# Gate and up projections of three four-tile blocks by seven block products instead of eight, on one core

## What is computed

```python
h = _rmsnorm(x, g_pre_mix) * (1 + sc1) + sh1
proj = h @ w_in                                  # 1024 -> 2176 columns, 17 units of 128
ya = pool_mixer(xa) ; yb = conformer_conv(xb) ; yc = short_conv(xc)
mix = jnp.concatenate([ya, yb, yc], axis=-1) @ w_out       # 1024 -> 1024
x = x + gt1 * _rmsnorm(mix, g_post_mix)
h = _rmsnorm(x, g_pre_ffn) * (1 + sc2) + sh2
f = (jax.nn.silu(h @ w_gate) * (h @ w_up)) @ w_down        # 1024 -> 2816 -> 1024
x = x + gt2 * _rmsnorm(f, g_post_ffn)
```

## Time and profile before

| | |
|---|---|
| median of 3 runs | 2252.78 us (2251.18 to 2254.14) |
| the profiled execution | 2248.84 us |
| its span, first to last instruction | 2247.1 us |
| mean granted TensorE clock | 0.999 |
| TensorE, VectorE, ScalarE busy | 99%, 61%, 45% of the span |
| DMA | 376.8 MB, mean 168 GB/s |

### The profile page before, as it was taken

One profiled execution on the slowest core, in us unless ns is written; L12 is line 12 of the kernel. 1 busy time (PEld: TensorE's weight loads), 2 busy tenths in 40 slices (PEclk: granted clock), 3 DMA queues, 4 the chain that ended last, 5 costly groups with the idle time before them and its releaser, 6 DMA issues.

```text
span 2247.1 us, 29845 instructions
## 1 busy us (share of the span) xinstructions
PE 2227.4 (99%) x12150; PEld 2057.5 (92%) x12150; DVE 1366.5 (61%) x1982; ACT 1004.6 (45%) x1419; POOL 37.0 (2%) x83
## 2 busy tenths in 40 slices
PE   9999999999999999999999999999999999999998
PEld 6779998979999988999898899989899998799987
DVE  3779966798444678644478854357884535443343
ACT  3455466454344544344444525354443424532332
POOL 0000000000000000000000000000000000000000
PEclk9999999999999999999999999999999999999999
DMA  9865654654543564544365363437435434744332
GB/s 376 311 218 169 237 205 142 187 180 168 169 157 125 175 162 131 182 151 155 126 196 147 124 214 122 152 130 205 133 131 178 124 130 154 183 152 158 124 129 94
DMA packets 165765, 376.83 MB, mean 168 GB/s; under 512 B 75351, under 2 KB 77527, under 8 KB 165116
## 3 DMA queue, kind: packets, MB, share of 16 engines
q1 hardware_dynamic: 165630, 374.93, 51.1%
HBM read 348.02 MB, written 19.00 MB: 163 GB/s over the span
## 4 chain that ended last, share of the span: by engine, by line
PE 89%; DVE 4%; DMA 1%; ACT 1%; issue 0%; SPq 0%; DVEq 0%; ACTq 0%
PE ps L711 88%; DVE wlo L1445 2%; DVE pr L1607 1%; DMA raw<-in_w_dn 1%; DMA raw<-in_w_mix 1%; DVE early L1607 1%; PE ps L741 0%; DVE g_lo L1508 0%; ACT whi L1038 0%; DMA raw<-in_w_gu 0%; DVE h_lo L1498 0%; SPq L528 0%; ACT h_f L1112 0%; DVE xt L1525 0%; ACT junk L1061 0%
## 5 line engine op out<-in xcount | busy, mean ns | idle before, releaser
L1445 DVE TENSOR_TENSOR wlo<-raw,whi 128x1024 fp32r<-128x1024 f32 x531 | 647.3, 1223 | 567.0 <-ACT whi L1038 565.3
L1038 ACT ACTIVATE whi<-raw 128x1024 fp32r<-128x1024 f32 x531 | 561.7, 1059 | 950.0 <-DMA raw<-in_w_gu 562.2
L711 PE MATMUL ps<-h_hi,whi 128*128 128x384 f32 (+1 forms) x2808 | 920.9, 328 | 1.8 <-DVE h_lo L1501 1.1
L711 PE MATMUL ps<-h_hi,wlo 128*128 128x384 f32 (+1 forms) x2808 | 919.3, 327 | 0.0
L711 PE MATMUL ps<-h_lo,whi 128*128 128x384 f32 (+1 forms) x2808 | 919.2, 327 | 0.0
L711 PEld LDWEIGHTS ps<-h_hi,whi 128*128 128x128 f32 x2808 | 528.6, 188 | 7.1 <-issue 4.7
L711 PEld LDWEIGHTS ps<-h_lo,whi 128*128 128x128 f32 x2808 | 528.6, 188 | 0.5
L711 PEld LDWEIGHTS ps<-h_hi,wlo 128*128 128x128 f32 x2808 | 528.6, 188 | 0.0
L711 PE MATMUL ps<-whi,g_hi 128*128 128x512 f32 x748 | 232.2, 392 | 5.9 <-DVE g_lo L1508 4.9
L711 PE MATMUL ps<-wlo,g_hi 128*128 128x512 f32 x748 | 230.5, 389 | 0.0
L711 PE MATMUL ps<-whi,g_lo 128*128 128x512 f32 x748 | 230.5, 389 | 0.0
(11 more groups left out here) (152 smaller groups left out, 1229.6 us busy)
## 6 DMA issues: line engine op xcount, KB each, us to landing
raw<-in_w_gu SPq DMA_DIRECT2D x264, 512.0 KB, 3.3
raw<-in_w_mix SPq DMA_DIRECT2D x150, 512.0 KB, 3.3
raw<-in_w_dn SPq DMA_DIRECT2D x132, 512.0 KB, 3.3
xr<-in_x_all SPq DMA_DIRECT2D x29, 512.0 KB, 6.0
xr<-x_all SPq DMA_DIRECT2D x17, 512.0 KB, 5.9
pre<-in_w_ada SPq DMA_DIRECT2D x16, 512.0 KB, 10.6
x_all<-xr SPq DMA_DIRECT2D x5, 1536.0 KB, 7.7
xt<-turn SPq DMA_DIRECT2D x80, 96.0 KB, 4.5
```

What stands on the lines that cost most here:

```text
L711: return nc.tensor.matmul(out, lhsT, rhs, start=start, stop=stop, skip_group_check=True)
L1038: nc.scalar.activation(whi[:, s, :], raw[:, s, :], ACT.Copy).then_inc(w_hi, 1)
L1445: tt(wlo[:, s, :], raw[:, s, :], whi[:, s, :].bitcast(F32), ALU.subtract).then_inc(w_lo, 1)
```

## The change

1. **Blocks.** `NT` = 2, 3, 4, 4, 4; five blocks. A block of four tiles has 512 columns. `RING` = 5, `LEAD` = 3. `IN_DOWN`, `IN_GATE_UP` and the places of the statistics change; a 512 column block of sums fills all eight banks.
2. **Gate and up of the four-tile blocks.** The 22 steps of two units become 11 pairs of seven products. A pair is two gate and two up column blocks; weights and activations are cut in two along the contraction (`KH` = 4 chunks) and the tokens in two (`HALF` = 256). Each of the seven products takes one unit of weights (a quarter of gate and of up, or one of four sums S1 to S4) and one of seven token combinations (`c_hi`, `c_lo`), 2 x 12 matmuls of 256 columns. Partial sums stay in three bank pairs (A, C, B) and go on accumulating; VectorE adds them (`r1`, `u2`, `u3`), ScalarE copies and does the silus.
3. **Weight sums.** While block 1 does gate and up, VectorE makes S1 to S4 from the raw units of two steps (`weight_sums`) and SP stores 2 MB for each pair (`store_sums`); the blocks 2 to 4 load them.
4. **Token combinations.** In the down projection before, ScalarE and VectorE make seven pairs `c_hi`, `c_lo` and four differences (`HIGH_AT`, `LOW_AT`), instead of eight `h_hi`, `h_lo`.
5. **FFN activations through memory.** The products go to `g_out`, SP stores them to `g_mem` and loads chunk by chunk into a ring of four (`load_g`), one 128x512 chunk beside each down unit.
6. **Pooling map folded.** s_pool, w_pool and the two units of w_out behind them are multiplied once (`fold_pool`), stored, and loaded as two units (`w_fold`); the two `w_pool` matmuls of each block and their copies go away. `norm_rows` moves from the output projection into the gate/up stage.

```diff
-TB = 3
-NT = [2, 3, 3, 3, 3, 3]
+TB = 4
+NT = [2, 3, 4, 4, 4]
+PRODUCTS = [("A11", "11", "A"), ("S2", "T2", "B"), ("S1", "T1", "C"), ("S3", "T3", "B"),
+            ("A12", "21", "A"), ("S4", "22", "C"), ("A22", "T4", "B")]
+CHAIN_BANK = {"A": 0, "C": 2, "B": 4}
-RING = 6
+RING = 5
-LEAD = 4
+LEAD = 3
-    STREAM += [("gu", c_, m_, i_) for m_ in range(NF) for i_ in range(2)]
+    if sliced(c_):
+        STREAM += [("sg", c_, p_, i_) for p_ in range(PAIRS) for i_ in range(NPROD)]
+    else:
+        STREAM += [("gu", c_, m_, i_) for m_ in range(NF) for i_ in range(2)]
-IN_DOWN = 3
-IN_GATE_UP = [6, 6, 6, 6, 6]
+IN_DOWN = [None, 1, 2, 3]
+IN_GATE_UP = [6, 3, 1, 1]
 def sum_bank(r, t):
-            return 0 if r == RES.index(("mix", NB - 1)) and t == 0 else 2 + 2 * t
+            return (0, 2, 6, 4)[t] if sliced(RES[r][1]) else 2 + 2 * t
+            def load_g(b, k):
...
+                if at >= G_LAND:
+                    sp.wait_ge(g_lo_ready, at - G_LAND + 1)
+                sp.dma_start(down_rings(b)[0][:, at % G_LAND, 0:w], g_mem[b % 2, k, :, 0:w]).then_inc(gf_landed[at % G_LAND], 16)
+            def fold_pool(p):
...
+                for h in range(2):
+                    last = mm(ps[:, 6 + h, :], w_pl[:, p, :], fold[:, p, 512 * h:512 * h + 512], True, True)
+            def product(b, p, i):
+                n, at = UNIT["sg", b, p, i], pair_at(b, p)
+                s, combo_at, f = n % RING, COMBOS.index(PRODUCTS[i][1]), norm("F", b)
+                for g in range(2):
...
+                    elif i == 0 and p:
+                        pe.wait_ge(g11_ready if g else s11_ready, at)
+                    elif i == 1 and p:
+                        pe.wait_ge(v21_ready, 2 * at - 1 + g)
+                    elif i == 2 and p:
+                        pe.wait_ge(v12_ready, 2 * at - 1 + g)
+                    elif i == 3:
+                        pe.wait_ge(u2_ready, 2 * at + 1 + g)
+                    elif i == 4:
+                        pe.wait_ge(r1_ready, 2 * at + 1 + g)
+                    elif i == 5:
+                        pe.wait_ge(v22_ready, 2 * at + 1 + g)
+                    elif i == 6:
+                        pe.wait_ge(u3_ready, 2 * at + 1 + g)
...
+                    for k in range(KH):
+                        w = slice((KH * g + k) * P, (KH * g + k + 1) * P)
+                        mm(out, whi[:, s, w], c_hi[:, combo_at, k, :], i < 3 and k == 0, False)
+                        mm(out, whi[:, s, w], c_lo[:, combo_at, k, :], False, False)
+                        last = mm(out, wlo[:, s, w], c_hi[:, combo_at, k, :], False, k == KH - 1)
+            def weight_sums(n):
+                _, _, m, e = STREAM[n]
+                n2 = UNIT["gu", SUMMED, m + 1, e]
...
+                elif e == 0:
+                    dve.wait_ge(sums_stored, 16 * p)
+                dve.wait_ge(w_landed[n % RING], landed(n))
+                dve.wait_ge(w_landed[n2 % RING], landed(n2))
...
+                at = own.step(tt(s1, a21, a22, ALU.add))
+                own.step(tt(s3, a11, a21, ALU.subtract))
+                after(at)
+                after(own.step(tt(s2, s1, a11, ALU.subtract)))
+                i = tt(s4, a12, s2, ALU.subtract)
             def low(n):
                 s = n % RING
+                if STREAM[n][0:2] == ("gu", SUMMED) and STREAM[n][2] % 2 == 0:
+                    weight_sums(n)
```

More of the change, by code:

```diff
@@ L57 @@
 NY1 = NPOOL + NSC
-RING = 6
+RING = 5
 G_RING = 3
-LEAD = 4
+G_LAND = 4
+LEAD = 3
 EARLY = 6
@@ L222, in tile_order @@
     kind, b = RES[r]
[L223 to L229, removed]
+    return {2: [0, 1], 3: [1, 0, 2] if kind == "ffn" else [0, 1, 2], 4: [0, 3, 1, 2] if kind == "ffn" else [0, 1, 2, 3]}[NT[b]]
+BY_TILE = [r for r in range(len(RES)) if sliced(RES[r][1])]
 def tile_ends(r, i):
-    return (NT[NB - 1] - 1) * BY_TILE.index(r) + i + 1
+    return (TB - 1) * BY_TILE.index(r) + i + 1
 def res_tile(r, t):
@@ L507, in source @@
                     return w_mix[key[2]]
+                if key[0] == "out" and Y[key[2]][0] == "g":
+                    return w_fold[Y[key[2]][1]]
                 if key[0] == "out":
@@ L576, in _ @@
                         sp.dma_start(w_pl[h:h + 64, g // 2, h:h + 64], w_pool[g]).then_inc(w_pool_landed, 16)
+                if j == 13:
+                    for p in range(NPOOL):
+                        sp.dma_start(fold[:, p, :], w_mix[NIN + Y.index(("g", p))]).then_inc(fold_landed, 16)
                 if j == 10:
@@ L627, in _ @@
                     load("out", c, k)
+                    if c and sliced(c - 1) and k == 6:
+                        store_pair(c - 1, PAIRS - 1)
+                    if c and not sliced(c - 1) and 2 <= k < 5:
+                        store_chunk(c - 1, NF - 5 + k)
+                    if c == SUMMED + 1 and k == 0:
+                        store_sums(PAIRS - 1)
                     if c == 0 and k == 1:
@@ new lines, in down @@
+                order = tile_order(r)
+                if ks[0] == 0 and sliced(b) and b < NB - 1:
+                    order = [0, 1, 2, 3] if b == NB - 2 else [1, 2, 3, 0]
+                by_rows(r, order, units, before)
+            def product(b, p, i):
+                n, at = UNIT["sg", b, p, i], pair_at(b, p)
+                s, combo_at, f = n % RING, COMBOS.index(PRODUCTS[i][1]), norm("F", b)
+                for g in range(2):
+                    if p == 0 and i < 3 and g == 0:
+                        r = RES.index(("ffn", b - 1))
+                        bank = CHAIN_BANK[PRODUCTS[i][2]]
+                        for t in range(NT[b - 1]):
+                            if sum_bank(r, t) == bank:
+                                pe.wait_ge(mix_read, res_tile(r, t))
+                        if not sliced(b - 1) and bank == 0:
+                            pe.wait_ge(evac_done, evac_count(b + 1, NIN - 1))
+                    elif i == 0 and p:
[12 more added lines that the diff above has]
+                        pe.wait_ge(u3_ready, 2 * at + 1 + g)
+                    if g == 0:
+                        if p == 0:
+                            pe.wait_ge(c_lo_ready, NPROD * combos_before(f) + combo_at + 1)
+                        wait_split(n)
+                    out = chain(i, g)
+                    for k in range(KH):
[3 more added lines that the diff above has]
+                        last = mm(out, wlo[:, s, w], c_hi[:, combo_at, k, :], False, k == KH - 1)
+                    last.then_inc(w_used if g else gate_full, 1)
@@ L1271, in _ @@
             ada_out(FOURS[7] // 2)
-            for c in range(NPOOL):
-                pooled_out(0, c)
             mean_out(0)
@@ L1915, in _ @@
+                    if m >= ROW_AT[c] and 4 * (m - ROW_AT[c]) < KD:
+                        for ch in range(4 * (m - ROW_AT[c]), 4 * (m - ROW_AT[c]) + 4):
+                            scale(norm("M", c + 2), ch)
                     w = NT[c] * P
```

752 lines of the change are left out of this document (571 added, 181 removed).

## The result

The change made the kernel slower: 2351.09 us median of 4 runs (2342.56 to 2351.85) against 2253.39 (2251.18 to 2254.14) of the kernel before, ratio 1.0432, 95% interval 1.0416 to 1.0447. The forecast was 2209, the range 2176 to 2245. The profiled execution has a span of 2349.0 us where the sum of the prediction gives about 2204.6, so 144 us have to be found.

A forecast was written before the change was run, and what follows sets the result against it. The prediction took TensorE's streamed columns, plus a few waits, to bound the kernel. Savings of -80.4 us and new waits summed to -44.2 us, giving 2209 us against the median 2252.8, range 2176 to 2245.

The forecast's parts named there:

- The columns: Gate and up of blocks 2, 3 and 4 as products of 256 columns: fewer columns for TensorE, -74.9 us.
- The rival of bank switches: Products' matmuls cost more because accumulation changes bank after 12: 0.003 us each, 17 us, total 2226; chance 0.03.
- (a): End of block 0's down projection: first weight sums wait for a unit loaded late, ahead of the split; +5 us (0 to 8).
- (b): Block 1's gate/up: VectorE waits for a pair's second unit, 2 us late in six rounds; +12 us (0 to 40).
- block 1 pays much more: Each round of block 1's sums waits out its whole store: 40 us instead of 12, total 2240; chance 0.13.
- (f): First 219 us: ring of five and the fold's 2 MB through the queue; +3 us (-1 to 12).
- (d): Three product phases: eight 2 MB transfers make weight landings late, by some 1 us; +8 us (0 to 30).
- (e): Blocks 2 and 3: bursts of ScalarE, from the variance with table loads and squares of four tiles; +3 us (0 to 12).
- the rival on landings: Product loop becomes bound by landings: gain gone at a landing of 6.1 us, 2299 us at 6.6 throughout; chance 0.07.
- (c): Projections after blocks 2 and 3: sums fill all eight PSUM banks, so the next projection starts late; +3.6 us (0 to 8).
- (g): Last down projection starts with no activation ready: silu, product, copy and split; +1.6 us (0 to 4).
- All new waits hidden: VectorE's slack hides every new wait: 2172 us, up to 2190 with some left; chance 0.15.

The follow-up runs named there:

- experiment 7: The change with its weight sums made from a copy of the first unit by ScalarE: 2310.05 us, ratio 1.0263 to the kernel before.
- experiment 12: The change with sums from a copy, stores in halves, moves of order and the residual tiles' load three units later: 2230.38 us, ratio 0.9911 to the kernel before.
- experiment 9: The change with sums from a copy and each pair's sums stored as two 1 MB halves: 2282.5 us, ratio 1.0135 to the kernel before.
- Experiment 2: The change with low halves of statistics sums ahead of splits in blocks 0 and 1, norm rows two pairs later: 2305.33 us, ratio 1.0232 to the kernel before.
- experiment 1: The change without making or storing weight sums, products reading units of the same size: 2261.05 us, ratio 1.0046 to the kernel before.
- experiment 4: The kernel before with only a ring of five unit slots in place of six: 2265.03 us, ratio 1.0068.
- experiment 6: The change without weight sums, with statistics, norm rows and the sixth strip load moved in order: 2231.36 us, ratio 0.9913 to the kernel before.

## Why the prediction was wrong, step by step

**The columns, -74.9: right.** The last product stage holds TensorE 223.6 us in 1,849 records, 0.1210 us each where the sum had 0.1201. The rival of bank switches falls too: its 0.003 us each would be 5.5 us in that stage, and busy time is 1.6 above the sum. The formula that the prediction quotes from the Trainium skill (TensorE: Matmul & The Clock Gate, section Back-to-back issue gap) is given there for an isolated matmul, without the weight load that stands before every one here; the measured 0.1210 us at 256 columns sides with the rows of before, as the prediction did.

**Block 0's down projection, -7.2: right, and covered at first.** In experiments 7 and 12 it took 59.8 us, and 264 x 0.2268 is 59.9. In the change the onset (a) ate it, in one wait of 5.2 us for `g_lo` where (a) has 5: 66.9 us, 2 above the forecast's 64.9.

**(b), weight sums in the loop, +12: the step that failed.** It let VectorE wait until "3.3 at best ... about 4.3", from median landings of before. In the chain the landing that the sums wait for took 5.3, 7.6, 10.2, 10.8 us. SP had issued 2 MB of sums or of tiles 1.3 to 6.1 us ahead of each; that these made it slow is likely by experiments 7 and 9, but no run took them away alone. The working also took one round as standing in place, 2 us late in six of eleven. But the load is released by TensorE's own progress, so a late round makes the next load late: it is a loop, with landing + sums + split + two units in it. The rival "block 1 pays much more" named this round, and its price (40, by one whole store each) stopped at waits. Where the sum had 12, block 1 took 76 us more than the 185.1 of its matmuls: 57 us of waits (34.2 for `wlo`, 22.7 for `y_pr`) and 19.5 of slower matmuls.

**No term for who else stands in VectorE's queue.** The low half of each statistics sum stands behind splits and sums: 36.4 us of waits for `y_pr`, up to 13.2 each. It was not in the sum at all. Experiment 2 took it down to 4.1 us. It was also there without sums (14.6 us in experiment 1); the ring of five alone brings 2.7 of it (experiment 4), and where the rest comes from stays open.

**No term for the clock.** TensorE was busy 2198.2 us, and 2163.7 in experiment 6 with the same 13,034 records: 34.5 us of slower matmuls, mean clock 0.973 against 0.995. So a wait is not paid once. That the lower clock follows the long waits is seen in the timeline above and in experiment 1, where block 1 had 1.7 us of waits and a clock of 1.00. It is no fixed price for each us waited: idle 151, 121, 102, 66 us in the change and experiments 7, 9, 6 went with busy 2198, 2183, 2182, 2164. Nor does the mean clock give the time by itself: one run of the kernel before has 0.948 at 2252.7 us, the others have 0.997 or more at 2248 to 2255 us.

**(f), ring of five and fold, +3: mis-sized.** 10.4 us in one wait by experiment 4, 8.7 in the change. I had bounded it by what landings do, and the cause was SP's order: a load released by TensorE stands ahead of one that is not.

**(d) and (e), products, +11: mis-sized.** Idle in the three stages is 22.3, 12.1 and 5.2 us. Of this, 8.3 are the norm rows, moved by the change to a pair where `rstd_x` is not ready, which the sum had no term for. The rest are adds (`r`) of 1 to 1.5 us late and statistics. In experiment 12 the three stages still take 714.0 us against 665.8 of product matmuls. Landings were not what bound them: medians of 3.7 us for the sums' units and 4.2 for the quarters, where the working allows 5.4. So the rival on landings (slower, 0.07) was on the right side for the wrong reason.

**The small terms** (c) and (g): of the size forecast. In the change TensorE waits 3.3 us for `xt` in two waits, where (c) has 3.6, and 2.3 us once for `g_lo_last`, where (g) has 1.6.

The prediction said that idle time over 80 us would prove it wrong; it was 151. "All new waits hidden", 2172 to 2190, was never reached: with most waits of order taken out the time is still 2230.

## What to carry to other kernels

Where an engine's queue waits for a transfer whose issue waits for the engine that is being fed, write the round down as a loop and compare its length with the work it feeds; a slack by sum says nothing. Before giving a queue a wait, list what stands behind it there, up to the smallest operation that another engine wants, and do the same for the queue that issues transfers: put what can go before what must wait. When several edits each look worth little, try them together, since only the longest round shows.

## What the runs showed of the hardware

A long wait of TensorE costs more than its length: in block 1 of the change 57 us of waits came with 19.5 us of slower matmuls (204.6 us busy at clock 0.89 against 185.1 at 1.00, experiment 1), and behind a wait of 9.57 us matmuls of 384 columns started 0.32 us apart where they had been 0.17.

A 512 KB load issued behind a 2 MB store landed after 8.3 to 10.1 us in eight rounds of experiment 7, and after 13.2 us in the first; the median in the kernel before was 3.3. The Trainium skill (DMA: Bandwidth & Descriptors, section Queues, rings and completion order) says that each DMA engine takes the descriptors of one ring in their order; by that rule the load starts behind the store's bytes, and the chain of experiment 7 agrees (8.45 and 10.05 us).

DMA traffic by itself did not hold block 1 of the change: the stage of experiment 12 moved 299 GB/s on average with a DMA share of 0.85 and ran at 190.6 us, while the change moved 221 GB/s and took 261.5.
